# Gated delta rule of a hybrid layer: decay rows in two parts, their broadcasts first, gate work one weight chunk sooner

## The chip, the cores and the metric

The kernel runs on one core of a Trainium2 chip. The metric is the device time of one execution in microseconds (us). The matrix engine (TensorE, PE in the rows), the vector engine (DVE), the scalar engine (ACT), GpSimd (POOL) and the queue that starts transfers (SP) run side by side and meet only at semaphores. A matrix product in plain fp32 stands in the trace as two matrix instructions, one in fp32r as one.

## What is computed

Two post-normalised layers of mixed attention and experts come first; then one hybrid layer, of which the gated delta rule and a recurrent unit (RG-LRU) are the mixers, and a feed-forward part. The change lies in the hybrid layer alone. There, with S = 512 tokens, 4 heads of 128 and, in the kernel, chunks of 128 tokens:

```python
h = rmsnorm(x, norm_mix_w)
proj = jnp.einsum("bsd,de->bse", h, w_in)            # q, k, v, z, beta, a, lru_x, lru_gate
qkv = jax.nn.silu(causal_depthwise_conv(qkv, gdn_conv_w))
q = l2norm(q); k = l2norm(k)
beta = jax.nn.sigmoid(b_logit)
g = -jnp.exp(gdn_A_log) * jax.nn.softplus(a_logit + gdn_dt_bias)
...
g_cum = jnp.cumsum(to_chunks(g), axis=-1)
diff = g_cum[..., :, None] - g_cum[..., None, :]
decay = jnp.where(causal, jnp.exp(jnp.where(causal, diff, 0.0)), 0.0)
k_beta = k * beta[..., None]
v_beta = v * beta[..., None]
a_low = jnp.where(strict, jnp.einsum("bhnid,bhnjd->bhnij", k_beta, k) * decay, 0.0)
rhs = jnp.concatenate([v_beta, k_beta * jnp.exp(g_cum)[..., None]], axis=-1)
sol = lax.linalg.triangular_solve(i_plus_a, rhs, left_side=True, lower=True)
qk_intra = jnp.where(causal, jnp.einsum("bhnid,bhnjd->bhnij", q, k) * decay, 0.0)
```

## The kernel before

The program is a row of stages, each closed by a barrier of all engines (`stage`, L73 and L76). Inside a stage each engine runs its own instructions in the order in which they are written. Three stages matter here.

**in_projection_2** projects the normalised input with `w_in_2`. The weights come in 12 chunks of 256 columns (`i` = 0 to 11), each of which gives two *units* of 128 output columns (u = 2i and 2i+1). A unit is 24 matrix instructions (L1752): 8 blocks of 128 rows by the three products in `TERMS`, since each operand is split in a high and a low fp32r part. The high part of a chunk is a copy on ACT (`high`, L1774), the low part a subtraction on POOL (L1931); both go to one of two buffers, so `high(i)` waits until unit 2i-3 is done. Beside the 24 units the matrix engine has a unit GATES (the gates' columns), one ROWS (16 small transposes that turn gate rows into columns, L1735) and eight SUM units: for each head of q and k the sum of squares, a product with ones (L1741) of what `square` (L1872) wrote. `order` fixes the sequence, and the unit at place n takes PSUM bank n mod 8, so that it waits until whoever empties the unit at place n-8 has done so (`free`). Units are emptied by ACT (`home`, L1778) or DVE (L1853), sums by ACT (`log_of`, L1809: the logarithm, followed by `inverse_of`, L1813, the exponential of minus a half of it). `scale` (L1889) multiplies q and k with the result. The gates' own work is small, 4 partitions by 512: `gate_rows` and `soft_gate` (L1796, L1797) and `gate_decays` (L1801, L1802) on ACT, `gate_sums` (L1876 to L1883, the scans of the cumulated decay among them) and BE (L1914) on DVE. A last step of POOL is a convolution for the recurrent unit (`recurrent_conv`, 7 instructions, L1946 to L1949).

**gdn_matrices** makes the operands of the solve. The matrix engine turns k and v of every chunk (L1979), then broadcasts three rows of each head, GC (cumulated decay), BT (beta) and EG (its exponential), over 128 partitions (L1986: a product of a one-hot column with a block of 4 rows, plain fp32, in four banks taken in turn), then multiplies k with KB and q (L1997, called the triangular products below). DVE makes KE, KD and VB from the turned chunks (L2011, L2012, L2015), then per head RM (L2019), KB (L2021), QE (L2023) and GL (L2025) from the broadcasts, and last AT and AQ (L2030) from the triangular products and from E, which ACT computes from RM (L2043). POOL does three more `recurrent_conv`, 21 instructions, which depend on nothing of this stage.

**gdn_inverse** solves the triangular system by doubling, in 7 levels: per level products (L2092, L2102) and transposes (L2095), with DVE and ACT emptying banks, and the recurrent unit beside it (gate products L2080; POOL's last step L2193). It begins with transposes of AT (L2084). The stage after it begins with L2206.

## Time and profile before

| | us |
|---|---|
| median of 3 runs | 2021.8 |
| lowest and highest | 2018.83 and 2023.35 |
| the profiled execution's own time | 2016.86 |
| its span from first to last instruction | 2015.0 |

A row of the timeline is: start in us, duration in us, engine, line, operation, what it writes and reads, shape, and the count of instructions merged in it; in brackets how long the engine had been idle before it and what ended that. PEld is the weight load of the matrix engine. Line numbers are those of the kernel before, and every time counts from the span's start. The hybrid layer's projection runs from 1275.7 to 1430.5 us, gdn_matrices from 1431.7 to 1465.2, gdn_inverse from 1466.5 to 1538.9.

### The profile page before, as it was taken

The numbers are of one execution on the slowest core, as the hardware profiler recorded it, in microseconds if no ns is written. First come the engines' busy times: TensorE is split into PE (matmuls) and PEld (weight loads), VectorE is DVE, ScalarE is ACT, GpSimd is POOL, SyncE is SP. The second block draws the span as 40 slices with busy tenths as digits, with TensorE's granted clock in tenths as the row PEclk, the third lists the DMA queues.
The fourth block names the chain that finished last, engine by engine and source line by source line (L and its number), as shares of the span: only waits on it lengthen the run. The fifth ranks groups of instructions, "written<-read, shape, count | busy, mean of one in ns | idle before, by whom it ended". The sixth has DMA issues, their size and how long they took to land. (4 is left out here: it accounts for less than half of the span.)

```text
span 2015.0 us, 22447 instructions
## 1 busy us (share of the span) xinstructions
PE 1720.0 (85%) x7998; PEld 1329.1 (66%) x7998; DVE 1131.6 (56%) x1702; ACT 886.2 (44%) x1326; POOL 634.0 (31%) x337
## 2 busy tenths in 40 slices
PE   5999897859971999997949991899996689999997
PEld 4876634648861886742837880687686578888885
DVE  4925565559956655646558985395454324323242
ACT  3246575248863235656337872435342331111111
POOL 2336622112210434731202210342812124344441
PEclk9999998969995999989969995899798899999998
DMA  5201111169944211020157972320000232222211
GB/s 186 81 32 44 38 48 63 41 269 347 378 187 179 105 53 44 1 69 17 61 240 302 372 287 113 140 100 17 20 1 1 84 126 84 105 94 94 104 62 52
DMA packets 40475, 233.84 MB, mean 116 GB/s; under 512 B 9316, under 2 KB 9700, under 8 KB 20660
## 3 DMA queue, kind: packets, MB, share of 16 engines
q1 hardware_dynamic: 31012, 215.44, 28.4%
q0 software_dynamic: 9216, 16.80, 2.3%
q8 instruction: 60, 0.98, 0.2%
q10 hardware_dynamic: 144, 0.26, 0.1%
q14 instruction: 43, 0.35, 0.1%
HBM read 226.01 MB, written 23.23 MB: 124 GB/s over the span
## 5 line engine op out<-in xcount | busy, mean ns | idle before, releaser
L258 PE MATMUL bank<-XS,WS 128*128 128x512 f32 x864 | 200.4, 394 | 11.8 <-DVE WS L383 10.2
L2435 POOL TENSOR_TENSOR WS<-ring,WS 128x2048 fp32r<-128x2048 f32 x31 | 149.5, 4824 | 188.4 <-ACT WS L2423 188.4
L258 PEld LDWEIGHTS bank<-XS,WS 128*128 128x128 f32 x864 | 164.3, 191 | 47.5 <-DVE WS L383 10.7
L1366 PE MATMUL bank<-WS,XS 128*128 128x512 f32 x768 | 189.7, 404 | 1.1 <-DVE XS L1486 1.1
L2423 ACT CAST WS<-ring 128x2048 fp32r<-128x2048 f32 x31 | 59.3, 1913 | 271.7 <-PE bank L2456 144.1
L2456 PE MATMUL bank<-XS,WS 128*128 128x512 f32 x768 | 174.9, 389 | 3.0 <-DVEq L2485 3.0
L2474 PE MATMUL bank<-WS,US 128*128 128x512 f32 x768 | 174.7, 389 | 0.0
L1366 PEld LDWEIGHTS bank<-WS,XS 128*128 128x128 f32 x768 | 146.4, 194 | 32.5 <-DVE XS L1486 1.9
L2456 PEld LDWEIGHTS bank<-XS,WS 128*128 128x128 f32 x768 | 144.1, 188 | 33.1 <-DVEq L2485 3.2
L2474 PEld LDWEIGHTS bank<-WS,US 128*128 128x128 f32 x768 | 144.1, 188 | 29.9
L1752 PE MATMUL bank<-XS,WS 128*128 128x512 f32 x576 | 138.2, 401 | 7.2 <-ACT XT L1809 3.3
L1752 PEld LDWEIGHTS bank<-XS,WS 128*128 128x128 f32 x576 | 111.0, 193 | 33.6 <-ACT XT L1809 4.1
L469 POOL TENSOR_TENSOR WS<-raw,WS 128x2048 fp32r<-128x2048 f32 x18 | 84.0, 4666 | 109.7 <-ACT WS L313 109.7
L677 POOL TENSOR_SCALAR XT<-XT,RC 128x512 f32<-128x512 f32 x64 | 100.0, 1564 | 47.0 <-DVE RC L642 46.8
L1329 POOL DMA_INDIRECT mixed_rows<-YE,table x32 | 33.4, 1044 | 242.4 <-DVE table L1503 167.6
L1390 PE MATMUL bank<-DS,HT 128*128 128x512 f32 x384 | 98.2, 405 | 6.3 <-DVE DS L1493 6.1
L2505 DVE TENSOR_TENSOR X<-X,bank 128x512 f32<-128x512 f32 x32 | 22.0, 687 | 144.4 <-PE bank L2474 144.4
L1480 DVE TENSOR_TENSOR WS<-raw,WS 128x2048 fp32r<-128x2048 f32 x32 | 73.1, 2290 | 29.1 <-ACT WS L1427 29.1
L1390 PEld LDWEIGHTS bank<-DS,HT 128*128 128x128 f32 x384 | 72.1, 193 | 21.5 <-issue 6.5
L995 PE MATMUL bank<-WS,XS 128*128 128x512 f32 x360 | 83.4, 391 | 0.0
L1931 POOL TENSOR_TENSOR WS<-ring,WS 128x2048 fp32r<-128x2048 f32 x11 | 53.7, 4881 | 87.3 <-ACT WS L1774 87.3
L313 ACT CAST WS<-raw 128x2048 fp32r<-128x2048 f32 x18 | 34.3, 1905 | 98.7 <-PE bank L258 98.7
(507 smaller groups left out, 3467.2 us busy)
## 6 DMA issues: line engine op xcount, KB each, us to landing
raw<-in_w_exp SPq DMA_DIRECT2D x16, 2048.0 KB, 13.7
DN<-in_w_exp SPq DMA_DIRECT2D x32, 1024.0 KB, 8.6
ring<-in_w_ff SPq DMA_DIRECT2D x32, 1024.0 KB, 4.8
raw<-in_w_in SPq DMA_DIRECT2D x20, 1024.0 KB, 4.8
GU<-in_w_exp SPq DMA_DIRECT2D x8, 2048.0 KB, 15.1
XT<-in_w_exp SPq DMA_DIRECT2D x8, 2048.0 KB, 15.3
ring<-in_w_in SPq DMA_DIRECT2D x12, 1024.0 KB, 4.8
raw<-in_w_out SPq DMA_DIRECT2D x8, 1024.0 KB, 4.8
```

What stands on the lines that cost most here:

```text
L258: last = pe.matmul(m.ps[g % 8][:, :], WS[:, i % 2, hw, at:at + P], XS[:, hx, k, :], start=(step == 0), stop=(step == 3 * KD - 1))
L469: pool.tensor_tensor(WS[:, i % 2, 1, :], m.raw[:, i % 4, :], WS[:, i % 2, 0, :].bitcast(F32), ALU.subtract).then_inc(w_low, 1)
L677: pool.tensor_scalar(PR[:, i % 4, :], PR[:, i % 4, :], a.RC[:, i % 4:i % 4 + 1], None, ALU.mult).then_inc(probs_normed, 1)
L995: last = pe.matmul(m.ps[2 * t + half][:, :], XS[:, hx, 4 * kh + k, t * P:(t + 1) * P], WS[:, 2 * kh + half, hw, k * S:(k + 1) * S], start= ...
L1366: last = pe.matmul(m.ps[2 + e % 2][:, :], r.XS[:, e % 2, hx, 4 * half + k, :], r.WS[:, half, hw, k * S:(k + 1) * S], start=(half == 0 and ...
L1390: last = pe.matmul(m.ps[5 + half][:, :], r.HT[:, hx, f * P:(f + 1) * P], r.DS[:, hw, at:at + S], start=(n == 0), stop=(n == 5))
L1480: dve.tensor_tensor(r.WS[:, half, 1, :], r.GU[e % 4][:, half * 4 * S:(half + 1) * 4 * S], r.WS[:, half, 0, :].bitcast(F32), ALU.subtract). ...
L1752: last = pe.matmul(bank[u][:, :], q.WS[:, i % 2, hw, at:at + P], b.XS[:, hx, k, :], start=(step == 0), stop=(step == 3 * KD - 1))
L2423: act.copy(f.WS[:, q % 2, 0, :], f.ring[:, q % 4, :]).then_inc(w_high, 1)
L2435: pool.tensor_tensor(f.WS[:, q % 2, 1, :], f.ring[:, q % 4, :], f.WS[:, q % 2, 0, :].bitcast(F32), ALU.subtract).then_inc(w_low, 1)
L2456: last = pe.matmul(m.ps[mine + u % 4][:, :], f.WS[:, q % 2, hw, k * 256 + c * P:k * 256 + (c + 1) * P], f.XS[:, hx, k, :], start=(n == 0), ...
L2474: last = pe.matmul(bank[:, :], f.US[:, hx, 4 * kh + k, t * P:(t + 1) * P], f.WS[:, q % 2, hw, k * S:(k + 1) * S], start=(kh == 0 and n == ...
```

## The change

1. In `in_projection_2` ACT's `soft_gate` and the logarithms of the first four sums move from chunk 9 to the end of chunk 8, ahead of the copy `high(9)` and of `home(16)`; `gate_decays` moves from chunk 10 to chunk 9. On DVE `gate_sums` moves ahead of the last two squares, and the column copy GN moves ahead of the last four `scale`. The unit ROWS goes from place 31 to place 29.
2. DVE writes each of the three rows in two fp32r parts (`split`): the rounded row on partitions 0 to 3 of RW, what is missing from it on partitions 32 to 35, and zeros between. SEL holds the one-hot columns for both. Six instructions at the stage's start clear and fill RW and SEL, and three times two write the rows.
3. In `gdn_matrices` a broadcast is one fp32r product over 36 partitions. They come sorted by kind, the four of GC ahead of the transposes, and DVE makes the four RM first, and after KE, KD and VB the four KB, then QE and GL.
4. Two tables (TAB, KTAB) are allocated in an inner scope, which makes room and moves no instruction.

```diff
-        order = [0, 1, GATES, ... SUM[6], SUM[7], 18, 19, 20, 21, ROWS, 22, 23]
+        order = [0, 1, GATES, ... SUM[6], SUM[7], 18, 19, ROWS, 20, 21, 22, 23]
...
                 elif 3 <= i <= 8:
                     silu(2 * i - 6)
                     silu(2 * i - 5)
+                    if i == 8:
+                        soft_gate()
+                        for c in range(4):
+                            log_of(c)
                 elif i == 9:
-                    soft_gate()
-                    for c in range(4):
-                        log_of(c)
                     for c in range(4):
                         inverse_of(c)
+                    gate_decays()
                 elif i == 10:
                     for c in range(4, 8):
                         log_of(c)
-                    gate_decays()
...
+            def split(n, row):
+                link(dve.tensor_copy(b.RW[R, n, :], row[R, :]))
+                link(dve.tensor_tensor(b.RW[32:32 + GH, n, :], row[R, :], b.RW[R, n, :].bitcast(F32), ALU.subtract))
+
+            for n in range(3):
+                link(dve.tensor_copy(b.RW[0:32 + GH, n, :], m.zeros[0:32 + GH, :]))
+            link(dve.tensor_copy(b.SEL[0:32 + GH, :], m.zeros[0:32 + GH, 0:GH]))
+            link(dve.tensor_copy(b.SEL[R, :], m.ident[R, R]))
+            link(dve.tensor_copy(b.SEL[32:32 + GH, :], m.ident[32:32 + GH, 32:32 + GH]))
...
             home(15)
+            gate_sums()
             for c in range(6, 8):
                 square(c)
-            gate_sums()
+            split(1, b.BT)
+            split(0, b.GC)
             home(17)
...
             dve.tensor_tensor(b.BE[R, :], b.BT[R, :], b.EG[R, :], ALU.mult).then_inc(rows_c, 1)
+            split(2, b.EG)
+            home(19)
+            dve.wait_ge(unit_done, place[ROWS] + 1)
+            dve.tensor_copy(b.GN[:, :], bank[ROWS][:, 0:64]).then_inc(home_dve, 1)
             for c in range(4, 8):
                 scale(c)
             home(21)
-            dve.wait_ge(unit_done, place[ROWS] + 1)
-            dve.tensor_copy(b.GN[:, :], bank[ROWS][:, 0:64]).then_inc(home_dve, 1)
...
+            def row_of(i):
+                n, h = divmod(i, GH)
+                if i >= 4:
+                    pe.wait_ge(row_used, i - 3)
+                pe.matmul(m.ps[4 + i % 4][:, :], b.SEL[0:32 + GH, h:h + 1].to_broadcast([32 + GH, P]), b.RW[0:32 + GH, n, :], start=True, stop=True).then_inc(row_done, 1)
+
+            for i in range(4):
+                row_of(i)
```

ACT in `in_projection_2`, from the silu of chunk 8 to the copy of chunk 10. The names are G for the gate rows, XT for the buffers of the inverse norms, EG and DK for the decays. Before:

```order
L1782 ACTIVATE QB<-QB 128x512 x2
L1774 CAST WS<-ring 128x2048
L1778 COPY LX<-bank 128x512
L1796 ACT_TABLE_LOAD
L1796 ACTIVATE G_6784<-G_6784 4x512
L1797 ACT_TABLE_LOAD
L1797 ACTIVATE G_6784<-G_6784 4x512
L1809 ACTIVATE XT<-bank 128x512 x4
L1813 ACT_TABLE_LOAD
L1813 ACTIVATE XT<-XT 128x512 x4
L1774 CAST WS<-ring 128x2048
```

And now:

```order
L1782 ACTIVATE QB<-QB 128x512 x2
L1796 ACT_TABLE_LOAD
L1796 ACTIVATE G_6784<-G_6784 4x512
L1797 ACT_TABLE_LOAD
L1797 ACTIVATE G_6784<-G_6784 4x512
L1809 ACTIVATE XT<-bank 128x512 x4
L1774 CAST WS<-ring 128x2048
L1778 COPY LX<-bank 128x512
L1813 ACT_TABLE_LOAD
L1813 ACTIVATE XT<-XT 128x512 x4
L1801 ACTIVATE EG<-GC 4x512
L1802 ACTIVATE DK<-G_6784 4x512
```

The gate functions and the four logarithms now stand ahead of the copy of chunk 9 (L1774) and the emptying of unit 16 (L1778), and the decays follow the first exponentials without a table load of their own.

DVE in `gdn_matrices`, from its first instruction. Before, the numbers kept:

```order
L2011 TENSOR_TENSOR KE_8076<-bank0,GN_6792 128x512
L2012 TENSOR_TENSOR KD_8077<-bank0,GN_6792 128x512
L2015 TENSOR_TENSOR VB_8078<-bank2,GN_6792 128x512
...
L2019 TENSOR_TENSOR RM_8067<-bank4,mask_54 128x512
L2021 TENSOR_TENSOR KB_8069<-bank5,QB_6793 128x512
L2023 TENSOR_TENSOR QE_8070<-bank6,QB_6793 128x512
L2025 COPY GL_8071<-bank6 128x4
```

And now:

```order
L2026 TENSOR_TENSOR RM_8093<-bank4,mask_54 128x512
L2026 TENSOR_TENSOR RM_8093<-bank5,mask_54 128x512
L2026 TENSOR_TENSOR RM_8093<-bank6,mask_54 128x512
L2026 TENSOR_TENSOR RM_8093<-bank7,mask_54 128x512
L2030 TENSOR_TENSOR KE_8102<-bank0,GN_6792 128x512
L2031 TENSOR_TENSOR KD_8103<-bank0,GN_6792 128x512
L2034 TENSOR_TENSOR VB_8104<-bank2,GN_6792 128x512
...
L2037 TENSOR_TENSOR KB_8095<-bank4,QB_6795 128x512
L2037 TENSOR_TENSOR KB_8095<-bank5,QB_6795 128x512
...
L2040 TENSOR_TENSOR QE_8096<-bank4,QB_6795 128x512
L2041 COPY GL_8097<-bank4 128x4
```

The four RM, which ACT needs for E, stand first, and the three instructions per head are sorted by kind behind the twelve from the turned chunks.

## Rows read from the trace of the kernel before

**Rows 1.** The page: busy time of the engines, share of the span, instructions

```profile
PE 1720.0 (85%) x7998; PEld 1329.1 (66%) x7998; DVE 1131.6 (56%) x1702; ACT 886.2 (44%) x1326; POOL 634.0 (31%) x337
```

**Rows 2.** Timeline, end of in_projection_2's chunk 8 to chunk 10

```profile
1367.82 1.15 ACT L1782 ACTIVATE QB<-QB 128x512 f32<-128x512 f32 x2
...
1374.34 1.88 PE L1741 MATMUL bank<-XT,ones 128*128 128x512 f32 x4
1374.59 1.90 ACT L1774 CAST WS<-ring 128x2048 fp32r<-128x2048 f32 x1 [5.62 <-PE bank L1752]
...
1375.65 6.05 PE L1752 MATMUL bank<-XS,WS 128*128 128x512 f32 x24
...
1376.57 4.61 POOL L1931 TENSOR_TENSOR WS<-ring,WS 128x2048 fp32r<-128x2048 f32 x1 [7.79 <-ACT WS L1774]
1376.68 5.05 DVE L1872 TENSOR_TENSOR XT<-QB 128x512 f32<-128x512 f32 x1
...
1381.54 1.88 PE L1741 MATMUL bank<-XT,ones 128*128 128x512 f32 x4
...
1382.34 1.28 ACT L1796 ACT_TABLE_LOAD   x1
...
1386.11 2.00 ACT L1809 ACTIVATE XT<-bank 128x512 f32<-128x512 f32 x4
1386.23 0.68 DVE L1876 SCALAR_TENSOR_TENSOR G<-GR,G 4x512 f32<-4x512 f32 x1 [2.88 <-ACT G L1797]
...
1386.73 7.35 PE L1752 MATMUL bank<-XS,WS 128*128 128x512 f32 x24 [3.32 <-ACT XT L1809]
...
1389.69 0.68 DVE L1883 TENSOR_TENSOR G<-GC 4x512 f32<-4x512 f32 x1
...
1393.92 1.88 PE L1741 MATMUL bank<-XT,ones 128*128 128x512 f32 x4
...
1395.23 22.37 PE L1752 MATMUL bank<-XS,WS 128*128 128x512 f32 x96
```

**Rows 3.** Windows: length; busy us of PE, PEld, DVE, ACT, POOL; granted clock, DMA share, GB/s

```profile
1387.60:1391.00 3.40, 3.40 (x10) 2.63 (x9) 2.60 (x6) 3.37 (x7) 0.00 (x0) 0.51 0.00 0
...
1431.70:1437.20 5.50, 5.46 (x32) 5.11 (x32) 4.42 (x7) 3.48 (x5) 5.16 (x4) 0.69 0.55 180
...
1442.20:1455.10 12.90, 11.98 (x15) 4.11 (x13) 6.76 (x14) 7.42 (x23) 12.07 (x10) 0.50 0.00 1
1455.10:1459.30 4.20, 4.13 (x19) 4.13 (x20) 1.02 (x3) 1.42 (x6) 3.92 (x4) 0.51 0.00 0
...
1464.50:1466.40 1.90, 0.01 (x1) 0.00 (x0) 0.69 (x1) 0.00 (x0) 0.00 (x0) 1.00 0.00 0
```

**Rows 4.** Timeline of gdn_matrices and the first instruction after it

```profile
1431.74 5.62 PE L1979 MATMUL bank<-ident,QB 128*128 128x128 f32 x32 [1.96 <-PEq L76]
...
1432.71 0.69 DVE L2011 TENSOR_TENSOR KE<-bank,GN 128x512 f32<-128x512 f32 x1 [2.21 <-PE bank L1979]
...
1440.41 0.68 DVE L2019 TENSOR_TENSOR RM<-bank,mask 128x512 f32<-128x512 f32 x1
...
1442.40 0.68 DVE L2019 TENSOR_TENSOR RM<-bank,mask 128x512 f32<-128x512 f32 x1
...
1455.17 2.08 PE L1997 MATMUL bank<-KB,QB 128*128 128x128 f32 x8 [0.98 <-DVE GL L2025]
...
1460.09 1.28 POOL L1949 TENSOR_TENSOR XT<-XT 128x512 f32<-128x512 f32 x1
...
1464.54 0.69 DVE L2030 TENSOR_TENSOR AQ<-bank,E 128x512 f32<-128x512 f32 x1
...
1466.49 1.94 PE L2084 MATMUL bank<-ident,AT 128*128 128x128 f32 x16 [1.98 <-PEq L76]
```

**Rows 5.** Timeline, the end of gdn_inverse and the start of the next stage

```profile
1531.68 7.24 POOL L2193 TENSOR_TENSOR XT<-QB,LG 128x512 f32<-128x512 f32 x4 [7.67 <-DVE QB L2138]
...
1539.85 5.16 PE L2206 MATMUL bank<-U,KE 128*128 128x128 f32 x24 [10.11 <-PEq L76]
```

More of the change, by code:

```diff
@@ L1690, in in_projection_2 @@
         SUM = [NU + 2 + c for c in range(8)]
-        order = [0, 1, GATES, *range(2, 15), SUM[0], SUM[1], 15, SUM[2], SUM[3], 16, SUM[4], SUM[5], 17, SUM[6], SUM[7], 18, 19, 20, 21, ROWS, 22, 23]
+        order = [0, 1, GATES, *range(2, 15), SUM[0], SUM[1], 15, SUM[2], SUM[3], 16, SUM[4], SUM[5], 17, SUM[6], SUM[7], 18, 19, ROWS, 20, 21, 22, 23]
         place = {u: n for n, u in enumerate(order)}
         bank = {u: m.ps[n % 8] for u, n in place.items()}
-        by_act = [0, GATES, 2, 4, 6, 8, 10, 12, 14, 16, *SUM[0:4], 18, *SUM[4:8], 20, 22]
-        by_dve = [1, 3, 5, 7, 9, 11, 13, 15, 17, 19, 21, ROWS, 23]
+        by_act = [0, GATES, 2, 4, 6, 8, 10, 12, 14, *SUM[0:4], 16, 18, *SUM[4:8], 20, 22]
+        by_dve = [1, 3, 5, 7, 9, 11, 13, 15, 17, 19, ROWS, 21, 23]
         emptied = {u: (home_act, n + 1) for n, u in enumerate(by_act)} | {u: (home_dve, n + 1) for n, u in enumerate(by_dve)}
@@ L1911, in _ @@
                 scale(c)
-            home(19)
             dve.wait_ge(rows_b, 1)
             dve.tensor_tensor(b.BE[R, :], b.BT[R, :], b.EG[R, :], ALU.mult).then_inc(rows_c, 1)
+            split(2, b.EG)
+            home(19)
+            dve.wait_ge(unit_done, place[ROWS] + 1)
+            dve.tensor_copy(b.GN[:, :], bank[ROWS][:, 0:64]).then_inc(home_dve, 1)
             for c in range(4, 8):
@@ L1956, in gdn_matrices @@
         dve_step, nat_done, nat_home, row_done, row_used, decay, tri_done, tri_home, ready, conv_step, gates_done, soft_step = sems
-        rows = [b.GC, b.BT, b.EG]
         @block.sync
@@ L1980, in _ @@
                     last.then_inc(nat_done, 1)
-            for h in range(GH):
-                for n in range(3):
-                    i = 3 * h + n
-                    if i >= 4:
-                        pe.wait_ge(row_used, i - 3)
-                    pe.matmul(m.ps[4 + i % 4][:, :], m.ident[0:GH, h:h + 1].to_broadcast([GH, P]), rows[n][0:GH, :], start=True, stop=True).then_inc(row_done, 1)
+            for i in range(4, 12):
+                row_of(i)
             pe.wait_ge(row_used, 12)
@@ L2006, in per_head @@
                 return b.GN[:, at:at + GH].rearrange("p (h a) -> p h a", a=1).to_broadcast([P, GH, P])
+            for h in range(GH):
+                dve.wait_ge(row_done, h + 1)
+                dve.tensor_tensor(blocks(w.RM[:, h, :]), blocks(m.ps[4 + h][:, :]), every_block(m.mask[:, 0, :]), ALU.add).then_inc(row_used, 1)
             for c in range(NT):
@@ L2016, in _ @@
             for h in range(GH):
-                i = 3 * h
-                dve.wait_ge(row_done, i + 1)
-                dve.tensor_tensor(blocks(w.RM[:, h, :]), blocks(m.ps[4 + i % 4][:, :]), every_block(m.mask[:, 0, :]), ALU.add).then_inc(row_used, 1)
-                dve.wait_ge(row_done, i + 2)
-                dve.tensor_tensor(w.KB[:, h, :], m.ps[4 + (i + 1) % 4][:, :], b.XC[:, 4 + h, :], ALU.mult).then_inc(row_used, 1)
-                dve.wait_ge(row_done, i + 3)
-                link(dve.tensor_tensor(w.QE[:, h, :], m.ps[4 + (i + 2) % 4][:, :], b.XC[:, h, :], ALU.mult))
-                dve.tensor_copy(w.GL[:, h, :], m.ps[4 + (i + 2) % 4][:, P - 1:S:P]).then_inc(row_used, 1)
+                dve.wait_ge(row_done, GH + h + 1)
+                dve.tensor_tensor(w.KB[:, h, :], m.ps[4 + h][:, :], b.XC[:, 4 + h, :], ALU.mult).then_inc(row_used, 1)
+            for h in range(GH):
+                dve.wait_ge(row_done, 2 * GH + h + 1)
+                link(dve.tensor_tensor(w.QE[:, h, :], m.ps[4 + h][:, :], b.XC[:, h, :], ALU.mult))
+                dve.tensor_copy(w.GL[:, h, :], m.ps[4 + h][:, P - 1:S:P]).then_inc(row_used, 1)
             for c in range(NT):
@@ L2040, in _ @@
             for h in range(GH):
-                act.wait_ge(row_used, 3 * h + 1)
+                act.wait_ge(row_used, h + 1)
                 for c in range(NT):
@@ L2562, in build @@
         m.IOTA = sb(nc, ctx, "IOTA", P, P)
-        m.TAB = sb(nc, ctx, "TAB", P, S)
-        m.KTAB = sb(nc, ctx, "KTAB", P, S)
         m.CC = sb(nc, ctx, "CC", P, 8)
@@ L2583, in build @@
             m.AUX = sb(nc, c1, "AUX", P, A_N)
+            m.TAB = sb(nc, c1, "TAB", P, S)
+            m.KTAB = sb(nc, c1, "KTAB", P, S)
             with ExitStack() as c0:
@@ L2725, in build @@
             b.GN = sb(nc, c1, "GN", P, 64)
+            b.RW = sbr(nc, c1, "RW", P, 3, S)
+            b.SEL = sbr(nc, c1, "SEL", P, GH)
             with ExitStack() as c2:
```

## The prediction

> **What bounds the kernel now.** I read the page first: the matrix engine is busy for 85% of the span [rows 1], so what the change can give are its waits and its slow stretches. Next I read the timeline of the stage the change touches first [rows 2]. One wait of the matrix engine stands out in it, 3.32 us on ACT's logarithm at L1809, and the rows above it show why: behind the copy of unit 16 ACT loads a table at 1382.34, runs the gate functions with a second load, and starts the logarithms at 1386.11, 3.77 us later; unit 17 needs the bank that the first of them empties. The reader should then look at the length of that unit: 7.35 us against 6.05 for the unit before. The granted clock says the same, 0.51 behind the wait, which is the 1.2 GHz level [rows 3].
>
> In gdn_matrices the timeline [rows 4] shows two chains. One runs through DVE and PE: turned chunks, broadcasts to 1455.1, triangular products from 1455.17, the last AQ at 1464.54 to 1465.23, and the next stage's first product at 1466.49. The other is POOL's convolutions, which wait for nobody and end at 1461.37 (1460.09 and 1.28). Now DVE's end decides, POOL is 3.86 us ahead of it.
>
> **Part 1, gates one chunk sooner.** Without the wait unit 17 starts 1.31 us behind the pair of sums at 1381.54 (that is the step from 1393.92 to 1395.23): at 1382.85 instead of 1386.73, so 3.88 us sooner. From unit 16's start to the sums behind it are 5.89 us, from unit 17's 7.19, so at full clock another 1.30 come off. Together 5.18 us. What follows is asked for again:
> - ACT's silu ends at 1368.97. With 3.77 for the gate functions and 0.5 for each of two logarithms it is at 1373.7, then waits for the second pair of sums (to 1376.22), and ends the fourth logarithm near 1376.7. `high(9)` queues behind that and slips from 1374.59 to 1376.7; so POOL's low part ends near 1383.4. Unit 18, its first user, starts at 1390.05 (1382.85, 5.89 and 1.31). Hidden, with 6.6 us to spare; past that each us is paid.
> - DVE: `gate_sums` takes 4.14 us (1386.23 to 1390.37) and now stands ahead of squares 6 and 7. It starts near 1376.7. POOL's subtraction stands in its way: a square of that kind took 5.05 us beside it and ended only after it, at 1381.73 [rows 2]. I take the whole 4.6 us as lost: 1376.7 + 4.14 + 4.6 = 1385.4, and the two squares of 0.7 end at 1386.8. PE asks for the first at 1382.85 + 5.89 = 1388.74. Hidden, by 1.9 us. If everything of `gate_sums` fell behind POOL, the squares would end at 1388.9, still no wait of weight.
> - Six instructions of `split` are of the size of L1876, 4x512, so 0.7 us at most each [rows 2]: two pairs come after the squares, and delay `home(17)` and `scale`, not a unit; the six that clear RW and SEL run at the stage's start, before DVE has a unit to empty. No row shows an fp32r copy of 36x512; between nothing and 4 us (six of 0.7), I take nothing, since the first unit alone lasts 5.9.
> - The last chunk: ACT's second round (a load, four logarithms, a load, four exponentials, near 6.8 us) starts behind unit 18's copy at about 1396.6, so `high(11)` runs from 1403.4 and POOL ends at 1409.9. Unit 22 would start near 1413.5, three units of 5.6 (22.37 for four) and the small ROWS behind 1395.6. Hidden by 3.6.
> - ROWS moved up waits for BE; that follows `scale(3)` on DVE at about 1397.9, and its place comes at 1401.2.
>
> **Parts 2 and 3, gdn_matrices.** With t0 for the stage's start (1431.74 in before), the first broadcast is usable after about 0.9 us, as the first turned block was (1432.71). From there DVE is never short of work. It does the twelve of KE, KD, VB in 7.70 us (1432.71 to 1440.41) and one head's RM, KB, QE and GL in 1.99 (1440.41 to 1442.40, the one round in which it hardly waits); together 0.9 + 7.7 + 4 x 1.99 = 16.6. The triangular products can start at t0 + 16.6 instead of t0 + 23.4: 6.8 us sooner. They and AT, AQ take 10.06 us (1455.17 to 1465.23), so DVE would be through at t0 + 26.7.
>
> But POOL ends at t0 + 29.63, since nothing of it changes and it starts with the stage. It becomes the last. From DVE's end to the next stage's first product are 1.26 us now; where POOL ends a stage, it was 0.93 (1538.92 to 1539.85) [rows 5]. So gdn_inverse starts at t0 + 30.56 instead of t0 + 34.75: 4.19 us are won, not 6.8. The same cover makes the one-pass broadcast nearly free of effect: 2.9 us of DVE's chain are slack, which also takes up a half clock under the triangular products, where the engine, idle before them, would run at 1.2 GHz as it does now (0.51 from 1455.1 to 1459.3).
>
> The price is idle time before gdn_inverse. PE is done near t0 + 26 and restarts at t0 + 30.6. An idle time of 1.98 us there left the clock at 1.00; one of 3.32 was followed by 0.51 [rows 2 to 4]. With over 4 us I expect the half level, for a time like that behind unit 17, where it cost 1.30. Bounds: nothing, and 2.1, half of the 4.2 us at 0.51 after 1455.1. The first products there wait partly for DVE, so I take 1.2. The Trainium skill (TensorE: Matmul & The Clock Gate, "Why this matters for your kernels") warns of idle gaps between bursts, behind which the engine is back at half rate; by it the 1.2 is paid, by the 1.98 us row alone it is not.
>
> **Sum.** -5.18 - 4.19 + 1.2 = -8.2 us. The profiled execution would go from 2016.86 to 2008.7; it lay 4.9 below the median, and the runs spread over 4.5. Set against the median, 2021.8 - 8.2 = 2013.6.
>
> **Rivals.**
> - *The clock holds before gdn_inverse.* For: the 1.98 us row. Against: the idle time more than doubles. -9.4, 2012.4 us.
> - *POOL is no bound*, so that the 6.8 comes through whole (with 1.26 behind it and no clock loss): -12.0, 2009.8 us. Against: 21 instructions whose durations nothing here touches.
> - *A new wait in the projection*: squares 6 and 7, or chunk 9, come late. A wait of w costs w and, past about 3 us, the clock again. For: DVE is held by POOL. Against: slacks of 1.9 and 6.6. A wait as long as the one removed, 3.3 us, gives -8.2 + 3.3 = -4.9, 2016.9 us.
> - *The change does not do what it says in gdn_matrices*: with 36 rows for 4 the broadcasts hold the clock low or run in more passes, DVE waits as before, and only part 1 counts, less the 2.1 us bound of the clock: -5.18 + 2.1 = -3.1, 2018.7 us.
> - *Slower: the half level stays in gdn_inverse.* In gdn_matrices it stayed at 0.50 from 1442.2 to 1455.1 though PE was busy 11.98 of 12.90 us [rows 3]. Those were broadcasts over 4 rows; gdn_inverse is products and transposes of 128x128. Each us of its work at half rate costs one, so after 9.4 us of work the gain is gone; if it lasted through 24 of the 65 us before its end [rows 4, 5], 2012.4 + 24 = 2036 us. Against: under the transposes at 1431.74 (32 in 5.62 us) and the products after 1455.17 the clock came back.
>
> The Trainium skill (same page, "Part 4: PE-mode transpose") says that transposes do not count as work for the clock, which would lengthen that half level. The trace does not bear it out: from 1431.7 to 1437.2 the matrix engine ran nothing but transposes, and the granted clock has a mean of 0.69, so it rose among them [rows 3].
>
> **Chances.** Forecast 0.55 (own range 2012.0 to 2015.5), clock holds 0.15, whole saving 0.05, new wait 0.15, little done 0.06, slower 0.04. A run of this kernel can tell 0.2%, 4 us, from no change. Of the new-wait case half stays faster; with 0.02 for scatter, faster is 0.55 + 0.15 + 0.05 + 0.07 - 0.02 = 0.80, same 0.16, slower 0.04. The range runs from the whole saving, 2009.8, to 2018.0, most of the new-wait case with the runs' scatter.
>
> **What would show it.** Right: no wait on the logarithm, unit 17 near 6 us, units 16 to 23 without a gap; in the next stage the first RM within 1 us, triangular products 16 to 17 us after the start, POOL's L1949 step the last to end, and 0.9 us behind it the first product of gdn_inverse, followed by some us at 0.5. Wrong: a wait on squares or on a low part between units 17 and 22, DVE ending gdn_matrices after POOL, or half clock in gdn_inverse past its second level.

## The result and the profile after

| | before | after |
|---|---|---|
| median of 4 runs each, us | 2020.81 | 2007.03 |
| lowest and highest | 2018.83 and 2023.35 | 2004.67 and 2009.59 |
| the profiled execution's own time | 2016.86 | 2004.67 |
| its span | 2015.0 | 2002.5 |

The ratio is 0.9941, with a 95% interval of 0.9924 to 0.9959: the changed kernel is faster, by 11.9 us at that ratio; the two medians are 13.8 us apart. The forecast was 2013.6 us and its range ended at 2009.8, so the result lies below both. Further runs of both kernels beside the experiments put the effect at 7.1 to 7.5 us. Both sizes of the effect have to be explained, and the gap between them too.

The page of the changed kernel, to be read beside [rows 1], has 12 matrix instructions fewer (twelve broadcasts in one instead of two) and 20.5 us less of PE's busy time:

```profile
PE 1699.5 (85%) x7986; PEld 1321.6 (66%) x7986; DVE 1135.2 (57%) x1714; ACT 886.2 (44%) x1326; POOL 634.0 (32%) x337
```

Timeline of the end of in_projection_2, the columns as in [rows 2]:

```profile
1371.52 0.60 ACT L1809 ACTIVATE XT<-bank 128x512 f32<-128x512 f32 x1 [0.26 <-PE bank L1741]
...
1372.01 1.90 ACT L1774 CAST WS<-ring 128x2048 fp32r<-128x2048 f32 x1
...
1373.15 6.12 DVE L1881 TENSOR_TENSOR_SCAN GC<-zeros,G 4x128 f32<-4x128 f32 x4
1373.98 4.57 POOL L1944 TENSOR_TENSOR WS<-ring,WS 128x2048 fp32r<-128x2048 f32 x1 [9.96 <-ACT WS L1774]
...
1378.12 6.05 PE L1752 MATMUL bank<-XS,WS 128*128 128x512 f32 x24
...
1380.66 1.29 DVE L1873 TENSOR_TENSOR XT<-QB 128x512 f32<-128x512 f32 x2 [0.21 <-DVE G L1884]
...
1384.01 1.88 PE L1741 MATMUL bank<-XT,ones 128*128 128x512 f32 x4
...
1385.33 11.48 PE L1752 MATMUL bank<-XS,WS 128*128 128x512 f32 x48
...
1391.71 0.67 DVE L1925 TENSOR_TENSOR BE<-BT,EG 4x512 f32<-4x512 f32 x1
...
1396.74 0.41 PE L1735 MATMUL bank<-ident,GM 4*128 4x4 f32 x4
...
1397.82 22.06 PE L1752 MATMUL bank<-XS,WS 128*128 128x512 f32 x96
```

The reader should see four things. The fourth logarithm (L1809) is over at 1372.12, long before unit 17 at 1378.12, which lasts 6.05 us where it was 7.35 [rows 2]. The two squares (L1873) end at 1381.95, and PE's sums, which need them, follow unit 17 without a wait; unit 18 starts at 1385.33. POOL's low part of chunk 9 ends at 1378.55, 6.8 us before unit 18. And BE is written at 1392.38, 4.4 us before ROWS (L1735) at 1396.74.

Timeline of gdn_matrices, as in [rows 4], and then the first product of gdn_inverse:

```profile
1421.85 1.46 PE L1990 MATMUL bank<-RW,SEL 36*128 36x512 f32 x4 [1.97 <-PEq L76]
...
1422.35 2.48 DVE L2026 TENSOR_TENSOR RM<-bank,mask 128x512 f32<-128x512 f32 x4 [1.74 <-PE bank L1990]
...
1433.16 2.58 PE L1990 MATMUL bank<-RW,SEL 36*128 36x512 f32 x4 [2.66 <-DVE KB L2037]
...
1438.13 2.07 PE L2013 MATMUL bank<-KB,QB 128*128 128x128 f32 x8 [2.38 <-DVE GL L2041]
...
1447.89 0.69 DVE L2046 TENSOR_TENSOR AQ<-bank,E 128x512 f32<-128x512 f32 x1
...
1450.21 1.26 POOL L1962 TENSOR_TENSOR XT<-XT 128x512 f32<-128x512 f32 x1
```

```profile
1452.58 3.64 PE L2100 MATMUL bank<-ident,AT 128*128 128x128 f32 x16 [4.73 <-PEq L76]
```

The triangular products (L2013) start 16.28 us after the stage's first product, where it was 23.43 [rows 4]. DVE's last AQ ends at 1448.58, and POOL's last convolution at 1451.47. The next product comes 1.11 us after POOL, and PE had been idle for 4.73 us before it.

Windows of the same kernel, columns as in [rows 3]: first the stage up to the triangular products, then two stretches of gdn_inverse:

```profile
1421.80:1438.10 16.30, 10.57 (x44) 7.19 (x44) 15.45 (x28) 13.13 (x33) 15.22 (x12) 0.73 0.17 61
1452.50:1456.20 3.70, 3.62 (x17) 3.65 (x18) 2.42 (x4) 0.00 (x0) 0.00 (x0) 0.50 0.02 4
1456.40:1461.00 4.60, 4.60 (x43) 4.60 (x42) 4.43 (x8) 1.65 (x3) 0.00 (x0) 0.97 0.00 0
```

In the first row DVE is busy 15.45 of 16.30 us and PE 10.57. The clock is 0.50, the 1.2 GHz level, for 3.7 us of gdn_inverse and 0.97 in the stretch behind.

An account by stage, from the matrix instructions of both timelines: the length of a stage runs from its first product to the next one's.

| us | before | after | difference |
|---|---|---|---|
| stages up to in_projection_2's first product | 1275.69 | 1273.79 | -1.90 |
| its first 48 products | 13.87 | 11.01 | -2.86 |
| from there to unit 16 | 86.09 | 86.12 | +0.03 |
| unit 16 to unit 18 | 19.58 | 14.41 | -5.17 |
| unit 18 to gdn_matrices | 36.51 | 36.52 | +0.01 |
| gdn_matrices | 34.75 | 30.73 | -4.02 |
| gdn_inverse | 73.36 | 74.88 | +1.52 |
| all that follows | 475.15 | 475.04 | -0.11 |
| span | 2015.0 | 2002.5 | -12.5 |

The three terms of the prediction are the rows of -5.17, -4.02 and +1.52. The two rows at the top, 4.8 us, belong to no term of it. The first 48 products of the stage, of before and then of after:

```profile
1275.69 14.03 PE L1752 MATMUL bank<-XS,WS 128*128 128x512 f32 x48 [2.92 <-POOLq L1928]
```

```profile
1273.79 11.18 PE L1752 MATMUL bank<-XS,WS 128*128 128x512 f32 x48 [3.15 <-POOLq L1941]
```

The granted clock of before in the first two stretches of these products, 0.52 and then 1.00, tells why they took longer; in after it was 1.00 from 1273.8 to 1284.8 us, which is all of them. The third row, the counterpart of the first window above, is used below:

```profile
1275.70:1282.00 6.30, 6.30 (x15) 4.96 (x16) 0.49 (x1) 2.26 (x2) 1.69 (x3) 0.52 0.82 316
1282.00:1289.50 7.50, 7.50 (x34) 6.12 (x33) 0.00 (x0) 0.59 (x1) 2.99 (x1) 1.00 0.81 317
1431.70:1455.10 23.40, 22.29 (x56) 11.19 (x56) 16.11 (x28) 11.92 (x28) 21.86 (x17) 0.65 0.13 43
```

### The profile page after: what moved, and what is told of

Its sections match the earlier page's. It is cut to its first block and busy times, and to the rows that moved or that the text cites. A ratio compares the mean times of both kernels' runs of the same rounds, so it can differ in the third digit from the quotient of the medians.

```text
span 2002.5 us, 22438 instructions
## 1 busy us (share of the span) xinstructions
PE 1699.5 (85%) x7986; PEld 1321.6 (66%) x7986; DVE 1135.2 (57%) x1714; ACT 886.2 (44%) x1326; POOL 634.0 (32%) x337
## 5 line engine op out<-in xcount | busy, mean ns | idle before, releaser
L258 PE MATMUL bank<-XS,WS 128*128 128x512 f32 x864 | 202.0, 396 | 11.8 <-DVE WS L383 10.2
L1752 PEld LDWEIGHTS bank<-XS,WS 128*128 128x128 f32 x576 | 107.9, 188 | 28.9 <-POOLq L1941 3.3
L1480 DVE TENSOR_TENSOR WS<-raw,WS 128x2048 fp32r<-128x2048 f32 x32 | 73.1, 2289 | 27.9 <-ACT WS L1427 27.9
```

What stands on the lines that cost most here:

```text
L258: last = pe.matmul(m.ps[g % 8][:, :], WS[:, i % 2, hw, at:at + P], XS[:, hx, k, :], start=(step == 0), stop=(step == 3 * KD - 1))
L1480: dve.tensor_tensor(r.WS[:, half, 1, :], r.GU[e % 4][:, half * 4 * S:(half + 1) * 4 * S], r.WS[:, half, 0, :].bitcast(F32), ALU.subtract). ...
L1752: last = pe.matmul(bank[u][:, :], q.WS[:, i % 2, hw, at:at + P], b.XS[:, hx, k, :], start=(step == 0), stop=(step == 3 * KD - 1))
```

## The experiments

Two questions stood open: is the surplus over 8.2 us a working of the change, and which edit does what. Theory A was the account of the prediction, with the surplus as scatter between executions, that of the clock above all, in places that the change does not touch. Theory B was that something else of the change, its new addresses or its order, gives the rest.

A table of all, each against runs of the kernel before on the same chip. The last four columns come from the profiled execution.

| kernel | median us (runs) | ratio, 95% interval | unit 16 to 18 | gdn_matrices | triangular products at | gdn_inverse |
|---|---|---|---|---|---|---|
| gates sooner alone | 2011.41 (12) | 0.9978, 0.9969 to 0.9987 | 14.40 | 35.76 | 24.74 | 73.36 |
| new order alone | 2016.76 (11) | 1.0003, 0.9991 to 1.0015 | 20.78 | 35.90 | 25.11 | 73.37 |
| split rows alone | 2015.11 (11) | 0.9992, 0.9983 to 1.0000 | 19.51 | 30.75 | 16.44 | 74.21 |
| tables moved alone | 2018.57 (11) | 1.0013, 1.0004 to 1.0022 | 20.78 | 35.78 | 24.87 | 73.36 |
| changed, again | 2009.31 (9) | 0.9965, 0.9950 to 0.9979 | 14.42 | 30.80 | 16.28 | 75.41 |
| changed, plain broadcasts | 2009.98 (12) | 0.9970, 0.9959 to 0.9981 | 14.40 | 34.88 | 23.57 | 73.37 |
| changed, a convolution later | 2004.59 (5) | 0.9946, 0.9930 to 0.9963 | 14.42 | 27.86 | 16.28 | 73.37 |
| changed, more products | 2009.64 (9) | 0.9962, 0.9947 to 0.9977 | 14.41 | 31.16 | 16.28 | 73.37 |
| later and old order | 2005.19 (6) | 0.9934, 0.9922 to 0.9947 | 14.41 | 28.67 | 16.46 | 74.56 |
| changed, third time | 2010.73 (5) | 0.9963, 0.9950 to 0.9976 | 14.41 | 30.78 | 16.28 | 74.57 |
| changed, fourth time | 2010.32 (5) | 0.9963, 0.9950 to 0.9976 | 14.42 | 30.75 | 16.30 | 74.93 |
| a convolution later, again | 2006.82 (6) | 0.9943, 0.9929 to 0.9958 | 14.41 | 27.84 | 16.28 | 73.38 |

The runs of before were 35 beside the first four kernels (median 2016.82), 23 beside the next four (2016.47) and 11 beside the last four (2018.16); together 69 runs from 2010.52 to 2023.78. Two single runs far above all others, 6128.7 us of gates sooner alone and 2681.2 us of tables moved alone, are in the counts and medians of the table and not in the ratios.

### The gates one chunk sooner, alone

The kernel before with part 1 of the change; the rows are not split.

```diff
-        order = [0, 1, GATES, ... SUM[6], SUM[7], 18, 19, 20, 21, ROWS, 22, 23]
+        order = [0, 1, GATES, ... SUM[6], SUM[7], 18, 19, ROWS, 20, 21, 22, 23]
...
+                    if i == 8:
+                        soft_gate()
+                        for c in range(4):
+                            log_of(c)
                 elif i == 9:
-                    soft_gate()
-                    for c in range(4):
-                        log_of(c)
...
+                    gate_decays()
...
+            gate_sums()
             for c in range(6, 8):
                 square(c)
-            gate_sums()
```

> Part 1 alone: gate functions and first four logarithms at the end of chunk 8, gate_sums ahead of squares 6 and 7, ROWS two places earlier; broadcasts and gdn_matrices as in the kernel before. Theory A (the change is worth what its stages lose, the rest of the measured 13.8 us is half-clock stretches elsewhere that come and go): unit 16's start to unit 18's start 14.4 us instead of 19.6, gdn_matrices still 34.75 us from its first product to that of gdn_inverse, the whole 5.2 us faster than before, ratio 0.9974. Theory B (something else in the change speeds up the stages ahead or the start of the projection, and lies in this part): 10 us or more faster, ratio 0.995 or less.

Measured: 0.9978, that is 4.4 us less (2.6 to 6.3). Timeline:

```profile
1378.15 6.13 DVE L1881 TENSOR_TENSOR_SCAN GC<-zeros,G 4x128 f32<-4x128 f32 x4
...
1381.80 1.88 PE L1741 MATMUL bank<-XT,ones 128*128 128x512 f32 x4
...
1383.12 6.05 PE L1752 MATMUL bank<-XS,WS 128*128 128x512 f32 x24
```

The sums at 1381.80 are those ahead of unit 17, which follows 1.32 us later and lasts 6.05 us: the wait is gone and nothing has come in its place. The whole effect agrees with the 5.18 us of the prediction. gdn_matrices took 35.76 us here against 34.75 in the profile of before, though no line of it is changed; the granted clock up to the triangular products was 0.59 here and 0.65 there. Such a difference of 1 us is the scatter of this account.

### The new order alone

The kernel before with the order of broadcasts and of DVE's work from the changed gdn_matrices, the broadcasts plain fp32 over the 4 rows.

```diff
-            for h in range(GH):
-                for n in range(3):
-                    i = 3 * h + n
-                    if i >= 4:
-                        pe.wait_ge(row_used, i - 3)
-                    pe.matmul(..., m.ident[0:GH, h:h + 1].to_broadcast([GH, P]), rows[n][0:GH, :], ...)
+            def row_of(i):
+                n, h = divmod(i, GH)
+                if i >= 4:
+                    pe.wait_ge(row_used, i - 3)
+                pe.matmul(..., m.ident[0:GH, h:h + 1].to_broadcast([GH, P]), (b.GC, b.BT, b.EG)[n][0:GH, :], ...)
```

> The new order of gdn_matrices alone, with the broadcasts as plain fp32 products over 4 rows; projection as before. Theory A: at half clock each broadcast takes 1.71 us, so the four RM wait for PE and QE waits again; gdn_matrices 32.3 to 35 us instead of 34.75, the whole 0 to 2.5 us faster. Rival (the order is what wins in this stage): 30.7 us as in the changed kernel, the whole 2.5 us faster with 1.5 us given back in gdn_inverse.

Measured: 1.0003 (0.9991 to 1.0015), no effect. The stage took 35.90 us, above the 32.3 to 35 that were expected, and far from the rival's 30.7. Timeline and, below it, the window of the stage up to the triangular products:

```profile
1436.21 0.69 DVE L2013 TENSOR_TENSOR RM<-bank,mask 128x512 f32<-128x512 f32 x1 [1.02 <-PE bank L1977]
...
1455.63 0.69 DVE L2027 TENSOR_TENSOR QE<-bank,QB 128x512 f32<-128x512 f32 x1 [0.82 <-PE bank L1977]
...
1458.28 2.08 PE L2000 MATMUL bank<-KB,QB 128*128 128x128 f32 x8 [0.98 <-DVE GL L2028]
```

```profile
1433.20:1458.20 25.00, 24.10 (x56) 12.10 (x56) 16.27 (x28) 13.05 (x33) 23.43 (x18) 0.58 0.12 40
```

DVE waits 1.02 us for a broadcast of the first kind and 0.82 for one of the last, and PE is busy for 24.10 of 25.00 us where DVE is for 16.27. The order only says on which of PE's products DVE waits.

### The split rows alone

The kernel before with the rows in two parts and the one-pass broadcast in the old order, the tables in the inner scope.

```diff
+            split(1, b.BT)
+            split(0, b.GC)
...
+            split(2, b.EG)
...
-                    pe.matmul(..., m.ident[0:GH, h:h + 1].to_broadcast([GH, P]), rows[n][0:GH, :], ...)
+                    pe.matmul(..., b.SEL[0:32 + GH, h:h + 1].to_broadcast([32 + GH, P]), b.RW[0:32 + GH, n, :], ...)
```

> The split alone: rows in two fp32r parts, one-pass broadcasts over 36 rows, in the old order behind the transposes and three per head; gates as before, tables in the inner scope. Theory A: a broadcast of 0.43 us or less is always ahead of DVE, DVE is through with GL at 16.6 us after the stage's start with either order, POOL ends the stage: 30.7 us, as in the changed kernel; in gdn_inverse 1.5 us are given back at half clock; the whole 2.5 us faster, ratio 0.9988. Rival (the broadcasts must also stand first): triangular products start later than 18 us after the stage's start and the stage takes over 31.5 us. Theory B for the rest: 6 us or more faster, if the moved tables or the split speed up other stages.

Measured: 0.9992 (0.9983 to 1.0000), 1.6 us less. Timeline and window as in the last experiment:

```profile
1438.72 5.36 PE L1997 MATMUL bank<-RW,SEL 36*128 36x512 f32 x8 [2.66 <-DVE RM L2030]
...
1446.07 2.08 PE L2008 MATMUL bank<-KB,QB 128*128 128x128 f32 x8 [1.99 <-DVE GL L2036]
...
1460.38 3.25 PE L2095 MATMUL bank<-ident,AT 128*128 128x128 f32 x16 [5.31 <-PEq L76]
```

```profile
1429.60:1446.00 16.40, 10.82 (x44) 6.25 (x44) 15.43 (x28) 9.81 (x23) 15.34 (x12) 0.79 0.18 60
```

Here the triangular products start after 16.44 us, as in the changed kernel, and the stage takes 30.75 us: the whole gain of the stage with nothing of the new order. PE's busy time up to there is 10.82 us and DVE's 15.43. The idle time before gdn_inverse (5.31 us) and its slow start (3.25 us for the 16 transposes, 1.94 in [rows 4]) are there too. In the account the two stages save 3.15 us together (108.11 to 104.96); the timed 1.6, with 0 to 3.4, is compatible with it and with the 2.5 us expected, and does not prove either.

### The tables moved alone

```diff
-        m.TAB = sb(nc, ctx, "TAB", P, S)
-        m.KTAB = sb(nc, ctx, "KTAB", P, S)
+            m.TAB = sb(nc, c1, "TAB", P, S)
+            m.KTAB = sb(nc, c1, "KTAB", P, S)
```

> Only the two tables TAB and KTAB move to the inner scope, so that every later tensor lies at another address; no instruction changes. Theory A: no difference, within 0.1%, and where the half clock falls differs from profile to profile. Theory B (addresses make the other 4 to 6 us): 4 to 6 us faster, ratio 0.9975.

Measured: 1.0013 (1.0004 to 1.0022), 2.6 us slower, with 0.8 to 4.4, where no difference was expected. So new addresses make nothing faster and theory B falls in that form. For the small loss I have no place: unit 16 to 18 and gdn_matrices took 2.2 us more than in the profile of before, but so they did with the new order alone, where no table moved.

### The changed kernel again, unchanged

> The changed kernel once more, unaltered. Theory A (half-clock stretches outside the two stages come and go between executions): this profile shows them at other places than the first; the start of in_projection_2, whose first 48 products took 11.0 us there and 13.9 in the profile of before, may show either; the two stages of the change as in the first profile (14.4 us from unit 16 to unit 18, 30.7 us for gdn_matrices, 74.9 for gdn_inverse), the whole 8 to 12 us faster than before. Theory B (systematic): 11.0 us again and 13 to 14 us faster.

Measured: 0.9965 (0.9950 to 0.9979), 7.1 us less. In this profile the first 48 products took 13.76 us, as in before, while unit 16 to 18 and gdn_matrices stood at 14.42 and 30.80. So the 2.86 us come and go without the change, and its own two stages repeat to 0.1 us, gdn_inverse to 0.5 (75.41):

```profile
1274.29 13.93 PE L1752 MATMUL bank<-XS,WS 128*128 128x512 f32 x48 [3.01 <-POOLq L1941]
```

Theory A is borne out against B, which had 11.0 us again and 13 to 14 in all; the 7.1 us are below the 8 to 12 that stood under A.

### The changed kernel without the split

The two parts of the rows, their setup and RW and SEL are gone, and the broadcasts are plain fp32 over the 4 rows, in the new order.

```diff
-                pe.matmul(..., b.SEL[0:32 + GH, h:h + 1].to_broadcast([32 + GH, P]), b.RW[0:32 + GH, n, :], ...)
+                pe.matmul(..., m.ident[0:GH, h:h + 1].to_broadcast([GH, P]), (b.GC, b.BT, b.EG)[n][0:GH, :], ...)
```

> The changed kernel without the split: broadcasts as plain fp32 products over 4 rows, in the new order. Theory A: gdn_matrices as with the order alone, 32.3 to 35 us against 30.7 with the split; the whole 1 to 3 us slower than the changed kernel. Rival (POOL's end hides the plain broadcasts too): 30.7 us, no difference.

Measured: 0.9970 (0.9959 to 0.9981), 6.0 us less. Timeline and window:

```profile
1451.89 2.07 PE L2001 MATMUL bank<-KB,QB 128*128 128x128 f32 x8 [0.98 <-DVE GL L2029]
...
1463.20 1.94 PE L2088 MATMUL bank<-ident,AT 128*128 128x128 f32 x16 [1.98 <-PEq L76]
```

```profile
1428.30:1451.90 23.60, 22.44 (x57) 11.03 (x57) 16.11 (x28) 13.11 (x33) 22.08 (x17) 0.65 0.13 42
```

The stage is back at 34.88 us, and PE is the busy engine (22.44 of 23.60 us, DVE 16.11). With the split alone at 30.75 this is the second half of the proof: the split is the whole gain of the stage and the order gives none. The split makes a broadcast cheaper at either clock, and with plain ones the clock is low for longer; no run separates the two. By an estimate from the rows of before, twelve plain broadcasts at the 0.86 us that they took at full clock and 5.6 us of transposes are 15.9 us, no more than DVE's 16.1, so much of what PE cost here is the half clock. What the split is worth in the end is less: stage and gdn_inverse together took 108.25 us here and 105.35 to 106.21 in the four profiles of the changed kernel, so 2.0 to 2.9 us. The times do not resolve it: 0.9970 here beside 0.9965 for the changed kernel, with intervals that overlap.

### The changed kernel with a convolution later

POOL's third convolution moves into gdn_inverse, behind the last copy of DVE's first level (T); PE waits for it before the gate products that read it.

```diff
-            for c in range(1, 4):
+            for c in range(1, 3):
...
+                if first == 2:
+                    pe.wait_ge(late_conv, 7)
...
+            pool.wait_ge(t_home, NT)
+            recurrent_conv(pool, Chain(pool, late_conv), m, b, 3)
```

> The changed kernel with POOL's third convolution (7 of its 21 instructions) moved from gdn_matrices to gdn_inverse, behind the first level there. Theory A (POOL's end sets the stage): POOL ends after 20 us, DVE ends the stage at 26.7, gdn_inverse starts at 28.0 instead of 30.7 us, the idle time of PE before it falls from 4.7 to about 2 us and with it the half clock there, so gdn_inverse takes 73.4 instead of 74.9; 2.7 to 4.2 us faster than the changed kernel. Rival (POOL is not what the barrier waits for): gdn_matrices stays at 30.7.

Measured: 0.9946 (0.9930 to 0.9963), 10.9 us less than before. Timeline:

```profile
1442.58 1.27 POOL L1962 TENSOR_TENSOR XT<-XT 128x512 f32<-128x512 f32 x1
...
1449.99 0.69 DVE L2046 TENSOR_TENSOR AQ<-bank,E 128x512 f32<-128x512 f32 x1
...
1451.93 1.94 PE L2102 MATMUL bank<-ident,AT 128*128 128x128 f32 x16 [1.98 <-PEq L76]
...
1458.11 0.77 POOL L1959 TENSOR_SCALAR XT<-LX,CP 128x512 f32<-128x512 f32 x1 [14.26 <-DVE T L2137]
```

POOL is through at 1443.85, DVE at 1450.68 and the next product comes 1.25 us behind DVE. The stage takes 27.86 us, 2.9 less than with POOL last, and after an idle time of 1.98 us PE does its 16 transposes in 1.94 us: gdn_inverse is back at 73.37. That POOL ends the stage in the changed kernel is shown by this; that the idle time in front of gdn_inverse costs the clock is borne out, and the next run takes it by itself.

### The changed kernel with more products

Behind the last triangular product PE does four plain fp32 products, 128x512, whose results nobody uses.

```diff
+            for n in range(4):
+                pe.matmul(m.ps[4 + n % 4][:, :], m.ones[:, :], m.X[:, 0, 0:S], start=True, stop=True)
```

> The changed kernel with four extra plain fp32 products of 128x512 (3.4 us at full clock, results unused) behind the triangular products, where PE is otherwise idle until POOL is done. Theory A (the idle time is what brings the half clock in gdn_inverse): gdn_matrices still 30.7 us, clock at 1.00 from the start of gdn_inverse, that stage 73.4 instead of 74.9, the whole 1.5 us faster than the changed kernel. Rival (the half clock comes for another reason): 74.9 again.

Measured: 0.9962 (0.9947 to 0.9977), as the changed kernel itself, where 1.5 us less was expected. Timeline:

```profile
1456.53 3.60 PE L2016 MATMUL bank<-X,ones 128*128 128x512 f32 x8
...
1458.46 1.26 POOL L1962 TENSOR_TENSOR XT<-XT 128x512 f32<-128x512 f32 x1
...
1461.21 1.94 PE L2102 MATMUL bank<-ident,AT 128*128 128x128 f32 x16 [1.09 <-PEq L76]
```

The idle time falls to 1.09 us, the transposes take 1.94 and gdn_inverse 73.37, so what PE does in those us ahead of gdn_inverse decides over the 1.2 to 2.0 us there: with 4.23 to 5.31 us of idle time gdn_inverse lost 0.9 to 2.0 us in all five profiles. The products end at 1460.13, 0.41 us past POOL, and the stage takes 0.4 more (31.16). The net gain in the account, 0.8 to 1.7 us, is below what these runs can show.

### The later convolution with the old order

The kernel with the later convolution and the order of before in gdn_matrices, all else of the change kept.

```diff
-            for i in range(4):
-                row_of(i)
...
-            for i in range(4, 12):
-                row_of(i)
+            for h in range(GH):
+                for n in range(3):
+                    ...
```

> The kernel with the third convolution late, but with the old order inside gdn_matrices: transposes first, then the one-pass broadcasts three per head. Here POOL no longer covers DVE's chain. Theory A (with one-pass broadcasts DVE is the bound in either order, so the new order wins nothing even uncovered): triangular products 16.3 to 16.6 us after the stage's start, gdn_matrices 27.9 to 28.2 us, no difference to the kernel with the new order. Rival (the order matters once POOL's cover is gone, because E comes later or the first broadcasts wait): 1 us or more longer than 27.9.

Measured: 0.9934 (0.9922 to 0.9947), 13.3 us less. It is the lowest ratio of all, but its interval overlaps those of the later convolution in the new order (0.9946 and 0.9943), and in the account it is 2.0 us behind that kernel (103.23 against 101.23 for the two stages). The stage was expected at 27.9 to 28.2 us by A and at 28.9 or more by the rival; 28.67 is neither. Timeline and three windows: under the triangular products, the idle time, and the transposes:

```profile
1444.72 2.07 PE L2009 MATMUL bank<-KB,QB 128*128 128x128 f32 x8 [1.99 <-DVE GL L2037]
...
1454.99 0.69 DVE L2042 TENSOR_TENSOR AQ<-bank,E 128x512 f32<-128x512 f32 x1
...
1456.93 3.13 PE L2098 MATMUL bank<-ident,AT 128*128 128x128 f32 x16 [1.98 <-PEq L76]
```

```profile
1444.50:1450.00 5.50, 5.28 (x24) 5.28 (x25) 1.55 (x3) 3.69 (x12) 3.35 (x3) 0.50 0.00 0
1455.00:1456.90 1.90, 0.00 (x0) 0.00 (x0) 0.68 (x1) 0.00 (x0) 0.00 (x0) 1.00 0.00 0
1456.90:1460.00 3.10, 3.07 (x17) 3.10 (x18) 2.34 (x4) 0.00 (x0) 0.00 (x0) 0.59 0.02 5
```

The triangular products start at 16.46 us, 0.18 later than in the new order; that is what the order is worth where POOL no longer covers it. The remaining 0.6 of the stage (28.67 against 27.86) lie under these products, at a clock of 0.50 in the 5.5 us from their start where the later convolution in the new order had 0.58. That is not the order's doing as far as is known: the same products took 10.23 us here, and 9.59 to 10.29 in the four profiles of the changed kernel, with one order. Here the clock was 1.00 in the idle time of 1.98 us, and the transposes still took 3.13 us, at a mean of 0.59: the same idle time, once with the clock kept and once with it lost.

### The changed kernel a third and fourth time, and the later convolution again

The changed kernel twice more and the kernel with the later convolution once more, none with a new edit, to tell the last 4 us between them.

> The changed kernel once more, for the size of the whole effect. Theory A (the two stages' 7.7 us are all of it; the first comparison, four runs a side, caught high runs of before and low ones of after): ratio 0.996 to 0.997, 6 to 8 us; projection's first 48 products anywhere from 11.0 to 13.9 us. Theory B (systematic): ratio 0.9941 again.

> As the run before it: the changed kernel, a further profile and comparison. Theory A: 6 to 8 us faster, ratio 0.996 to 0.997. Theory B: 0.9941.

> The changed kernel with POOL's third convolution late, once more. Expected 4 to 5 us faster than the changed kernel in the same comparison (2.9 us from gdn_matrices, 1.5 from the clock in gdn_inverse), ratio to before 0.9945; gdn_matrices 27.9 us and gdn_inverse 73.4.

Measured: 0.9963 both times (0.9950 to 0.9976, 7.5 us less), and 0.9943 (0.9929 to 0.9958, 11.5 us less). The later convolution is 4.7 us faster than the changed kernel in the first pair of medians and 3.7 in the second. The account gives 4.1 to 5.0 (stage and gdn_inverse together 101.23 us against 105.35 to 106.21). In the last profile 3.5 us of it were lost again behind gdn_inverse, where all that follows took 478.68 us and 474.61 to 476.52 in the thirteen others; that is more of the scatter outside the change.

## Why the prediction was right, and where it was wrong

- **The wait on the logarithm and the half clock of unit 17** (5.18 us): right, 5.17. Without the change unit 16 to 18 took 19.51 to 20.78 us in four profiles, with it 14.40 to 14.42 in ten. The match to 0.01 us rests on the profile of before: unit 17 took 7.35 us in it and 8.55 in two others of the same code, where the change would have been worth 6.4.
- **DVE beside POOL**: the four scans took 6.12 us beside POOL's 4.57, 1.75 in before, so 4.37 are lost where the prediction took 4.6. By the Trainium skill (SBUF — State Buffer, "Who interferes with whom") a vector instruction with two inputs in SBUF and a GpSimd instruction that reads there contend with each other; the trace agrees, the scans lost nearly as long as the subtraction ran (4.57). The squares were 2.1 us ahead (1.9 said).
- **The covers**: chunk 9's low part was 6.8 us early (6.6 said), chunk 11's, over at 1405.37, 3.5 before unit 22 at 1408.85 (3.6 said), BE ahead of ROWS by 4.4 (3.3 said). The six instructions that clear and fill RW and SEL took DVE 1.8 us at the stage's start and cost nothing that shows: the first 48 products took 11.01 us with them, and from there to unit 16 the account has +0.03.
- **POOL as the new end of gdn_matrices** (-4.19): right, -4.02. The triangular products came at 16.28 (16.6 said), DVE was through at 26.73 (26.7), POOL at 29.62 (29.63), and the step to the next product was 1.11 instead of 0.93, which is the missing 0.17. The rival that POOL is no bound fell with that, and the later convolution showed what was to be had past POOL. Without the split the stage took 34.75 to 35.90 us in five profiles, so here too the close match rests on the profile of before.
- **The clock of gdn_inverse** (+1.2): right in kind, 1.52 here and 1.21, 1.57 and 2.05 in the other three profiles. The rival that the clock holds fell. Of the Trainium skill's two statements, the one on idle gaps (TensorE: Matmul & The Clock Gate, "Why this matters for your kernels") did as it says, 4.73 us of idle and then 0.50; the one on transposes ("Part 4: PE-mode transpose") was not borne out: the stretch begins with 16 transposes and was over within 3.7 us.
- **The slower rival**: it fell. The half level lasted 3.7 us of gdn_inverse, not 24.
- **The new wait in the projection**: it fell. Units 17 to 22 follow each other without a wait on any engine.
- **"The same cover makes the one-pass broadcast nearly free of effect"**: wrong, and the error of mechanism in this prediction. With the new order and plain broadcasts the stage took 34.88, with one-pass broadcasts and the old order 30.75. The step that failed is "From there DVE is never short of work", which was taken to hold whatever a broadcast costs: I had the 16.6 us from DVE's rows alone, and priced a head at 1.99 us, which held in one round only: PE had begun the broadcasts at 1437.29, while DVE was still at VB, and had filled its banks ahead. In the third round DVE waited for PE:

```profile
1445.69 0.69 DVE L2019 TENSOR_TENSOR RM<-bank,mask 128x512 f32<-128x512 f32 x1 [0.82 <-PE bank L1986]
```

In the rows of before the stretch up to the triangular products has PE busy for 22.29 of 23.40 us and DVE for 16.11, and [rows 3] already showed it in their stretch to 1455.1, 11.98 of 12.90 for PE and 6.76 for DVE. I read that row for its clock and not for who is busy. The sum came out since the change has both parts, and with one-pass broadcasts DVE is the busy engine (15.45 of 16.30 us). Had only the order been changed, the same working would have forecast 4.19 us, and the result, by the new order alone, was nothing.
- **The time itself**: wrong, 2007.03 for 2013.6, and below the range. The step that failed is the last, "Set against the median, 2021.8 - 8.2 = 2013.6". The median of three runs stood 4.9 us above the profiled execution, and it was the wrong one of the two: 69 further runs of before have medians of 2016.5, 2016.8 and 2018.2, so the base was 3.6 to 5.3 us too high. From the profiled execution the working gave 2008.7, and the four medians of the changed kernel are 2007.0, 2009.3, 2010.7 and 2010.3. The rest of the 6.6 us by which the time was missed is that the first four runs of the changed kernel were 2.3 to 3.7 us below its later medians, which nothing in the prediction could give, against an effect about 1 us smaller than forecast. Set beside the four runs of before of the same comparison (2020.81), 1.0 us of the miss is the base and 5.6 are the effect, 13.8 for 8.2; that this is scatter and no effect is what the three later comparisons say. The second fault is the low end, the whole saving without any scatter of the runs, while the high end had it. The effect was right in size: -8.2 said, -7.1 and twice -7.5 measured, and -7.7 in the three rows of the account. The account is no sharper than the times: taken from before or from the kernel with the moved tables, whose code in these stages is the same, to each of the four profiles of the changed kernel, the same three rows give 7.1 to 10.2 us.

The surplus of the first comparison, 11.9 for 7.1 to 7.5, is most likely not in the change: of the 12.5 us between the two spans 4.8 lie in two places that move about as much between executions of equal code, 2.86 of them at a granted clock of 0.52 in before. In the four profiles of the changed kernel the first 48 products took 11.01, 13.76, 11.04 and 11.04 us, and they started at 1273.79, 1274.29, 1275.24 and 1276.48. That the four timed runs of before were higher for this reason is not shown, since the profiled execution (2016.86) is none of them.

Open too: where the 2.6 us of the moved tables lie, if they are there.

## What to carry to other kernels

To find what bounds a stretch, set the busy times of all its engines beside each other in one window before costing a chain from one engine's rows: the engine that was 95% busy here was PE, and the best round of another engine's timeline does not show how fast the stretch can go. When a chain is shortened, read off what ends second, and look for what can be moved behind the barrier; here one convolution that nothing in the stage needs, moved, was worth 3.7 to 4.7 us more. And take the base from as many runs as there are, with their scatter at both ends of the range, above all where the profiled execution lies outside the three runs that give the median.

## What was unexpected of the hardware

- Plain fp32 broadcasts over 4 rows took 1.71 us each at a granted clock of 0.50, though PE was busy nearly all the time [rows 3]; the first of them had taken 0.86 at full clock. The one-pass ones over 36 rows took 1.19 us for four at full clock, in the split-alone kernel at 1434.87 us. In the five profiles with plain broadcasts the mean clock of the stretch up to the triangular products was 0.58 to 0.65, in those with one-pass ones 0.62 to 0.79.
- The same stage of the same kernel starts at half or at full clock in different executions: 13.76 and 11.04 us for the first 48 products.
- An idle time of 1.98 us in front of the same 16 transposes kept the clock in seven profiles (1.94 us, six kernels) and not in an eighth, of a seventh kernel (3.13 us), so the idle time just before a stretch does not tell its clock by itself.
